# Expert weights of a mixture layer: one load per pair of chunks instead of one per chunk

## The reference, cut to what matters

```python
def block_fn(args):
    xb, e = args
    h = jax.nn.silu((xb @ w_gate[e]).astype(f32)) * (xb @ w_up[e]).astype(f32)
    return h.astype(dt) @ w_down[e]
```

## Time and profile before

| | us |
|---|---|
| median of 3 runs (1915.17 to 1923.42) | 1921.36 |
| the profiled execution, its own time | 1921.21 |
| its span in the trace | 1919.5 |
| TensorE busy / VectorE / ScalarE / GpSimd, share of the span | 93% / 54% / 41% / 26% |
| mean granted clock of TensorE, share of full speed | 0.971 |
| weights of the experts: 192 loads of 1024 KB | 201 of 316 MB moved |

### The profile page before, as it was taken

The page is one execution under the profiler, slowest core; times in us unless marked ns, Lnnn a source line. Parts: engine busy times, 40 slices in busy tenths (PEclk is TensorE's granted clock), DMA queues, the critical chain, the costliest instruction groups (busy, mean ns, idle before and its releaser), DMA issues. The chain is left out here.

```text
span 1919.5 us, 25622 instructions
## 1 busy us (share of the span) xinstructions
PE 1778.6 (93%) x10100; PEld 1551.7 (81%) x10100; DVE 1041.5 (54%) x1192; ACT 781.8 (41%) x943; POOL 503.9 (26%) x285
## 2 busy tenths in 40 slices
PE   5999999999999999999999979929999999999992
PEld 5999989998999999999999968717777776667661
DVE  5555680001455444554511143256898887888884
ACT  5455460000122111221300032226787877778774
POOL 1323332223222322222222210022333332224210
PEclk9999999999999999999999989959999999999996
DMA  4211011223111111111132466327999999999995
GB/s 130 61 50 50 28 56 57 78 67 112 47 36 33 36 37 45 36 33 36 47 101 90 156 206 227 148 96 260 374 379 368 373 374 359 365 362 380 373 331 196
DMA packets 146085, 316.17 MB, mean 165 GB/s; under 512 B 10652, under 2 KB 106092, under 8 KB 121292
## 3 DMA queue, kind: packets, MB, share of 16 engines
q1 hardware_dynamic: 136140, 288.27, 41.7%
q0 software_dynamic: 9856, 26.66, 5.2%
HBM read 287.46 MB, written 35.29 MB: 168 GB/s over the span
## 5 line engine op out<-in xcount | busy, mean ns | idle before, releaser
L220 PE MATMUL job_ps<-xn_hi,w_hi 128*128 128x352 f32 x1536 | 511.6, 333 | 7.9 <-ACT ret_v_features L1017 4.7
L222 PE MATMUL job_ps<-xn_hi,w_lo 128*128 128x352 f32 x1536 | 494.9, 322 | 0.0
L221 PE MATMUL job_ps<-xn_lo,w_hi 128*128 128x352 f32 x1536 | 494.5, 322 | 0.0
L220 PEld LDWEIGHTS job_ps<-xn_hi,w_hi 128*128 128x128 f32 x1536 | 290.0, 189 | 11.6 <-issue 7.9
L204 POOL CAST w_hi<-w_raw 128x1024 fp32r<-128x1024 f32 x80 | 88.2, 1103 | 784.8 <-issue 465.9
L221 PEld LDWEIGHTS job_ps<-xn_lo,w_hi 128*128 128x128 f32 x1536 | 290.5, 189 | 2.3
L222 PEld LDWEIGHTS job_ps<-xn_hi,w_lo 128*128 128x128 f32 x1536 | 289.9, 189 | 0.0
L2054 DVE TENSOR_TENSOR ex_w_lo<-u,ex_w_hi 128x2048 fp32r<-128x2048 f32 x96 | 217.8, 2285 | 26.2 <-ACT ex_w_hi L1964 26.2
L2054 DVE TENSOR_TENSOR ex_w_lo<-h_raw_more,ex_w_hi 128x2048 fp32r<-128x2048 f32 x96 | 217.8, 2286 | 20.5 <-ACT ex_w_hi L1964 20.5
L206 POOL TENSOR_TENSOR w_lo<-w_raw,w_hi 128x1024 fp32r<-128x1024 f32 x80 | 215.5, 2693 | 6.4
L1964 ACT ACTIVATE ex_w_hi<-u 128x2048 fp32r<-128x2048 f32 x96 | 184.2, 1921 | 71.2 <-DMA u<-in_w_chunks 27.3
(11 more groups left out here) (279 smaller groups left out, 3049.4 us busy)
## 6 DMA issues: line engine op xcount, KB each, us to landing
u<-in_w_chunks SPq DMA_DIRECT2D x96, 1024.0 KB, 16.6
h_raw_more<-in_w_chunks SPq DMA_DIRECT2D x96, 1024.0 KB, 17.1
w_raw<-in_w_in SPq DMA_DIRECT2D x64, 512.0 KB, 4.1
merged_lru<-gate SPq DMA_DIRECT2D x8, 528.0 KB, 4.7
spare<-merged_lru SPq DMA_DIRECT2D x8, 528.0 KB, 5.5
merged<-gate SPq DMA_DIRECT2D x8, 528.0 KB, 4.8
x_tile<-in_x_prompt SPq DMA_DIRECT2D x8, 512.0 KB, 4.7
w_raw<-in_w_lru_o SPq DMA_DIRECT2D x8, 512.0 KB, 3.9
```

The lines of the kernel that those rows point to most:

```text
L220: pe.matmul(out, M.w_hi[s][:, k, :], x_hi[:, k, cols], start=(k == 0), stop=False)
L221: pe.matmul(out, M.w_hi[s][:, k, :], x_lo[:, k, cols], start=False, stop=False)
L222: mm = pe.matmul(out, M.w_lo[s][:, k, :], x_hi[:, k, cols], start=False, stop=(k == KD - 1))
```

## The change

The host lays out `w_chunks[e, j]` for j = 0 to 2, each [128, 4096] float32: the two chunks of one matrix side by side, 2 MB with 16384 contiguous bytes for each partition. One load brings a pair. The ring of eight chunk buffers stays in place and is seen as four pairs, each with one semaphore. A pair is loaded when VectorE is done with both chunks of the pair that was there. Everything that uses a chunk (ScalarE, VectorE, TensorE) still goes chunk by chunk and in the same order; only ScalarE's wait names the pair's semaphore.

```diff
@@ output projection, SyncE
-                    if t - 2 < Chunks.RAW:
-                        load_chunk(sp, A, H, *Chunks.ORDER[t - 2], t - 2)
-                for c in range(NTILE - 2, Chunks.RAW):
-                    load_chunk(sp, A, H, *Chunks.ORDER[c], c)
+                    if t % 2 == 0:
+                        load_pair(sp, A, H, t // 2 - 1)
@@ class Chunks
+    PAIRS = RAW // 2
-def load_chunk(sp, A, H, e, c, n):
-
-    b = n % Chunks.RAW
-    sp.dma_start(H.raw[b], A["w_chunks"][e, c]).then_inc(H.raw_in[b], 16)
+def load_pair(sp, A, H, n):
+
+    e, c = Chunks.ORDER[2 * n]
+    sp.dma_start(H.pair[n % Chunks.PAIRS], A["w_chunks"][e, c // 2]).then_inc(H.pair_in[n % Chunks.PAIRS], 16)
@@ experts, SyncE
-                for n in range(RAW, N_CHUNKS):
-                    sp.wait_ge(lo_done, n - RAW + 1)
-                    load_chunk(sp, A, H, *Chunks.ORDER[n], n)
-                    if n == RAW:
+                for n in range(PAIRS, N_CHUNKS // 2):
+                    sp.wait_ge(lo_done, 2 * (n - PAIRS) + 2)
+                    load_pair(sp, A, H, n)
+                    if n == PAIRS:
@@ experts, ScalarE
-                    act.wait_ge(H.raw_in[n % RAW], 16 * (n // RAW) + 16)
+                    act.wait_ge(H.pair_in[n // 2 % PAIRS], 16 * (n // RAW) + 16)
@@ class Routed
-        self.raw_in = [ctx.enter_context(nc.semaphore(f"raw_in{c}")) for c in range(Chunks.RAW)]
+        self.pair = [x[:, c * CHUNK_W:(c + 2) * CHUNK_W] for x in (R.u, self.more) for c in (0, 2)]
+        self.pair_in = [ctx.enter_context(nc.semaphore(f"pair_in{c}")) for c in range(Chunks.PAIRS)]
@@ host
+    chunks = chunks.reshape(E, 3, 2, P, CHUNK_W).transpose(0, 1, 3, 2, 4).reshape(E, 3, P, 2 * CHUNK_W)
```

More of the change, by code:

```diff
@@ L1662, in experts @@
         ps = lambda n, s: ctx.enter_context(nc.psum_tensor(f"ex_{n}", s, F32))
-        SPLIT, RAW, AT, N_CHUNKS = Chunks.SPLIT, Chunks.RAW, Chunks.AT, len(Chunks.ORDER)
+        SPLIT, RAW, PAIRS, AT, N_CHUNKS = Chunks.SPLIT, Chunks.RAW, Chunks.PAIRS, Chunks.AT, len(Chunks.ORDER)
         y_prompt, y_sample, conv_p, lru_p, conv_s, lru_s = outs
```

## The result

The changed kernel takes **1934.13 us** (median of 5 runs, 1933.26 to 1941.87) against 1921.34 us in 5 runs of the kernel before: the ratio is 1.0087, with a 95% interval of 1.0063 to 1.0111. It is slower. The five runs fall in two groups, 1933.3 to 1934.1 and 1941.6 to 1941.9; why, no run tells. The profiled execution (1941.56 us, span 1939.8) is of the upper one, so its numbers overstate the loss: its span is 20.3 us over that of before.

What follows compares the result with a forecast made beforehand. It took the never-empty weights' DMA queue to bound the experts, plus a tail. 1921.2 - 4.9 (longer packets) + 1.9 (tail) = 1918 us, all other terms 0; range 1905 to 1950 us.

Steps and rivals of the forecast that it cites:

- What bounds the kernel now: Experts, 1365 to 1876 us: the weights' DMA queue never empties, needing some 18.7 us per expert against TensorE's 17.66; 18.6 us lost.
- Longer packets: Weight loads of the experts: packets of 16384 B instead of 8192 B save 0.18 us per expert, -4.9 us in all.
- Half as many transfers: Weight loads: a transfer's fixed part is not on the path, as three pairs stand in the queue; nothing taken.
- The first chunk of a pair is ready with the second: Weight ring: first chunk ready and reissued 2.94 us later; nothing while the queue is full, +1.9 us in the tail.
- Rows beside longer packets: Gathers and stores beside weight loads: 1.8 us more per landing, bounds 0 to 4.6; 0 taken, as the queue decides.
- The threshold: Loop of store, gather and transpose: it decides once a step passes 18.7 us, from 3.3 us growth of both landings' sum.
- x: Growth of a store's and a gather's landing summed, over two steps; a step becomes 17.66 + (x - 1.2) / 2; 3.6 estimated.
- B: Rival: the gather is late in the first stretch only, 1365 to 1577 us; +4 us, 1925 us; chance 0.17.
- rule of turns: DMA engines: each serves its queues in turn, a whole packet at a time; six longer packets add 1.8 us per landing.
- C: Rival: the rows' loop becomes the bound; 1946 us for twelve steps, 1974 us for all 27; chance 0.25.
- the room after 1577 us: Later experts: gathers land in 9.0 us and GpSimd waits 5.99 us before a store; held against the rows' loop binding.
- D: Rival: the weights' queue gains much more, leaving TensorE's pace; -18.6 + 1.9, 1905 us; chance 0.15.

## Why the prediction was wrong

The time came out at 1934.13 us, in the range but on the other side of the 1918 forecast. Point by point:

- **What bounds the kernel now** was right: a queue of weights that never empties, with the rows beside it. Spreading the rows took 16.1 us away (0.84%), and that the fullest engines set the queue's end fits. But the 18.6 us that I read as lost to it were not all its own: 4.9 of them are the one step of 22.53 us, in which TensorE waits for VectorE's work for the router and then for its own clock. With spread rows the 27 steps take 482.9 us instead of 495.4; most of the rest of the gain lies behind the last expert's first gate matmul. That slots lie six to an engine stays an estimate; no run fixes the number, and the trace does not tell the engines apart.
- **Longer packets, -4.9 us: wrong.** Alone, 56 packets of 16384 B take 1.069 x 32 / 56 = 0.611 us, as worked out:

```profile
q1 hardware_dynamic: 56, 0.92, 106.9%
```

  (changed kernel, queue from 1318 to 1320 us). But beside rows nothing is gained. From 1400 to 1550 us the weights' queue shows, in the kernel before and in the changed one:

```profile
q1 hardware_dynamic: 7186, 52.33, 90.6%
```

```profile
q1 hardware_dynamic: 3452, 50.25, 87.3%
```

  That is 41.6 and 41.7 us of packet time for each MB (0.906 x 16 x 150 / 52.33). The runs with the loop cut confirm it: no gain from length.
- **Half as many transfers, nothing: right.** Pairs in one transfer with short packets (1.0015) and the same two chunks in two transfers, issued and taken up in twos (1.0019), take the same time. The fixed cost of about 2.0 us in the Trainium skill (DMA: Bandwidth & Descriptors, Anatomy of one DMA) does not show as time of the queue here. The section gives it for DMAs issued by GpSimd and lays most of it to the wait for the completion, so it did not speak for a gain of 164 us.
- **The first chunk of a pair is ready with the second: wrong place.** The forecast was nothing on the way and +1.9 us in the tail. Measured are 3 us on the way and no tail. ScalarE's last two high parts in the changed kernel, beside the earlier trace rows, wait for TensorE and not for a landing:

```profile
1894.49 1.92 ACT L1963 ACTIVATE ex_w_hi<-h_raw_more 128x2048 fp32r<-128x2048 f32 x1 [0.86 <-PE ex_up L1838]
1897.39 1.92 ACT L1963 ACTIVATE ex_w_hi<-h_raw_more 128x2048 fp32r<-128x2048 f32 x1 [0.98 <-PE ex_y L1838]
```

  Pairs with short packets, where the queue decides, have no tail either: their last two high parts start at 1874.73 and 1877.62 us, both behind a wait for TensorE. The step "while the queue is full neither moves the queue's end" failed. That the later take-up lets single engines run dry is the likely cause, since a ring of six costs too and since even engines make the cost vanish; it is argued, not shown.
- **Rows beside longer packets: the step that decided, and it failed.** "I take 0 for the forecast: the queue decides" was wrong. The threshold was named, 3.3 us; the growth from 1500 to 1577 us is 3.3 for a store and 1.7 for a gather, x = 5.0. By the formula a step would be 19.56 us; 18.63 were seen. The difference is the copy ahead of the gather, 0.18 us instead of 2.12, as the "against" of B had thought possible: 17.66 + (5.0 - 1.2 - 1.94) / 2 = 18.6. The prediction's 1.8 us for each landing is right for a store that has the queue to itself (2.1); it left out that store and gather are in one queue, so that a longer gather pushes the store behind it, as read above from their landings.
- **The Trainium skill's rule of turns** (DMA: Bandwidth & Descriptors, Queues, rings and completion order) was set down as speaking against the change and then weighed by the step it would give. The runs now agree with turns: 4, 8 and 16 KB, 8.3, 10.0 and 13.6 us. What takes a turn here is one packet of the profile, a partition's run of bytes. The section calls 9 to 17 descriptors a typical packet; the runs do not bear out a turn of that length, since a load of 2 MB in packets of 8192 B holds up a store no more than one of 1 MB (9.8 and 10.0 us).
- **The rivals.** C happened, with 0.25. Its mechanism is the one shown, over all of the experts and not in the first stretch alone: TensorE waits for rows up to 1876 us. Its price was too high: 1946 to 1974 forecast, 1934 measured (1941.6 in the profiled execution), for the copy, and since in some steps the landings were short again. What I held against it, the room after 1577 us, did not hold: that room came with TensorE's longer steps, 18.9 to 19.9 us from 1577 to 1674 us, and went with the waits for chunks that had made them. B and D did not happen.

The account of the 12.8 us by medians: about 3 for the pair, about 2 within the uncertainty of any of these runs, and 7.4 for the loop.

## What to carry to other kernels

Beside a stream of large packets a small indirect transfer pays for their length (stores of 8.3, 10.0 and 13.6 us here): look for a chain that hangs on such a landing, and work out its slack against the packet, before lengthening packets that already run at full rate. When the slack is small, cut the chain first (here four more row lists of one column). And a DMA share of 1.0 is no proof of full use: see whether the work is even over the engines; here another order of the slots was worth 16 us.

## What was not expected of the hardware

- Loads of 64 neighbouring partitions (0 to 63, 64 to 127) run their packets at half rate (1.18 us for 16384 B, 223 GB/s with all else that moves); loads of every other partition run at full rate.
- Where 16384 B alone took 0.611 us and 2 x 8192 B 0.618, beside rows the time for a MB is the same to 0.4%.
- GpSimd's copy of a row list takes from 0.18 to 2.3 us, and the gather's issue from 1.00 to 3.2 us, depending on when they come. For the copy the traces show with what: all six long ones of the kernel before from 1410 to 1510 us end 0.04 us after an instruction of VectorE, and those of 0.18 us in the changed kernel have none beside them. The copy that ran from 1467.69 to 1469.81 us stood beside

```profile
1467.48 2.28 DVE L2054 TENSOR_TENSOR ex_w_lo<-u,ex_w_hi 128x2048 fp32r<-128x2048 f32 x1
```

  which ends at 1469.76. So by this reading 1.94 of its 2.12 us were waiting and not work, and a shift of the copy took them away. No run changes VectorE's order to try it.
- A wait of TensorE of about 3 us is followed by a fall of its granted clock to half for 3.4 us, at 1474 us in the changed kernel and at 1686 us in the kernel before, so that it costs about half as much again.
